# Where the first head's query weights wait, and how closely two blocks' units are set among the expert rows

## The reference, cut to what matters

```python
xn   = rmsnorm(x)                                    # x: 1024 tokens x 1024
proj = xn @ w_in                                     # columns of both branches and their gates
mix  = (sigmoid(g_sb) * y_sb @ W_sb + sigmoid(g_ml) * y_ml @ W_ml) @ w_out
h    = x + mix                                       # y_sb: stick-breaking attention, y_ml: mLSTM
# PEER: experts by product keys
q        = (rmsnorm(h) @ w_query).reshape(T, 8, 2, 128)
v1, i1   = top_k(q[:, :, 0] @ keys1[h].T, 16)        # 8 heads, 128 keys per half
v2, i2   = top_k(q[:, :, 1] @ keys2[h].T, 16)
top_s, c = top_k(v1[..., :, None] + v2[..., None, :], 16)
e        = i1[c // 16] * 128 + i2[c % 16]            # 8 heads x 16 = 128 experts per token
out      = h + sum_k softmax(top_s)_k * gelu(expert_u[e_k] . hn) * expert_v[e_k]
```

## Time and profile before

| | us |
|---|---|
| median of 3 executions | 3257.53 (3256.76 to 3258.34) |
| the profiled execution's own time | 3256.99 |
| its span, first to last instruction | 3254.8 |
| TensorE busy | 2583.9 (79%) |
| VectorE busy | 2067.9 (64%) |
| ScalarE, GpSimd busy | 1132.3, 1208.8 |
| moved by DMA | 1258.39 MB, 387 GB/s over the span |

### The profile page before, as it was taken

How to read it: one execution, slowest core, us unless ns; L and a number is a source line. 1 busy time by engine, 2 the same in 40 slices (tenths; PEclk the granted TensorE clock), 3 DMA queues, 4 the chain that set the end, 5 groups by cost and what they waited for, 6 DMA issues and landing times.

```text
span 3254.8 us, 40512 instructions
## 1 busy us (share of the span) xinstructions
PE 2583.9 (79%) x14592; PEld 1309.4 (40%) x14592; DVE 2067.9 (64%) x4792; ACT 1132.3 (35%) x3556; POOL 1208.8 (37%) x1048
## 2 busy tenths in 40 slices
PE   8997988998898788997787887899787555555555
PEld 6775544555364243553353333455353111111111
DVE  1324659777458788764448798775447857765544
ACT  3211435442323553332323474334132232233222
POOL 0002334333334453333334365333333444444443
PEclk9998999999999999999899999999998777777777
DMA  4455999999999999999999999999999999999998
GB/s 137 138 180 195 411 415 388 416 416 417 389 411 418 412 419 417 415 419 417 416 412 403 413 401 420 416 418 414 417 415 413 402 421 421 421 419 418 421 420 333
DMA packets 219287, 1258.39 MB, mean 387 GB/s; under 512 B 24272, under 2 KB 27344, under 8 KB 88016
## 3 DMA queue, kind: packets, MB, share of 16 engines
q0 software_dynamic: 147456, 1073.81, 80.1%
q1 hardware_dynamic: 64128, 161.56, 13.5%
q10 hardware_dynamic: 7504, 20.45, 1.6%
HBM read 1249.96 MB, written 5.77 MB: 386 GB/s over the span
## 4 chain that ended last, share of the span: by engine, by line
DMA 41%; PE 34%; DVE 9%; issue 6%; ACT 6%; POOL 3%; DVEq 0%; POOLq 0%; ACTq 0%; SPq 0%
DMA rowsb<-uv,e_idx 38%; PE yacc L975 13%; PE mixp L622 7%; DVE rowsb L1820 4%; PE mixp L647 4%; POOL rowsb L1046 3%; DMA wt<-w_query_ 3%; PE mixp L720 2%; ACT diag L1365 2%; ACT wg L1360 2%; PE mixp L634 1%; PE yacc L622 1%; DVE area L1464 1%; PE mixp L659 1%; ACT gmt L1346 1%
## 5 line engine op out<-in xcount | busy, mean ns | idle before, releaser
L1046 POOL DMA_INDIRECT rowsb<-uv,e_idx x1024 | 1204.6, 1176 | 2019.0 <-PE yacc L975 1583.3
L1820 DVE CUSTOM_DVE_ANT_0 rowsb<-rowsb,hnrow 128x1024 f32<-128x1024 f32 x1024 | 1242.1, 1222 | 843.7 <-DMA rowsb<-uv,e_idx 838.7
L975 PE MATMUL yacc<-rowsb,diag 64*64 64x512 f32 x8192 | 1196.0, 707 | 606.8 <-ACT diag L1365 587.7
L975 PEld LDWEIGHTS yacc<-rowsb,diag 64*64 64x64 f32 x8192 | 295.0, 148 | 1337.1 <-ACT diag L1365 908.7
L1346 ACT ACTIVATE gmt<-dots 128x2 f32<-128x2 f32 x512 | 104.1, 203 | 1585.5 <-DVE dots L1820 1571.5
L622 PE MATMUL mixp<-area,wt 128*128 128x256 f32 x2112 | 488.6, 385 | 1.3 <-ACT area L1101 1.2
L622 PEld LDWEIGHTS mixp<-area,wt 128*128 128x128 f32 x2112 | 392.6, 190 | 131.7 <-issue 82.8
L1365 ACT ACTIVATE diag<-ident,wg 128x64 f32<-128x64 f32 x1024 | 300.3, 340 | 16.7
L1360 ACT ACTIVATE wg<-gmt,gate 128x1 f32<-128x1 f32 x1024 | 245.5, 286 | 17.7
L647 PE MATMUL mixp<-area,wt 128*128 128x256 f32 x960 | 225.5, 388 | 6.4 <-DMA wt<-w_query_ 6.3
L1064 ACT ACTIVATE area<-mixp 128x512 f32<-128x512 f32 (+3 forms) x314 | 136.9, 482 | 268.2 <-PE mixp L622 136.8
(11 more groups left out here) (257 smaller groups left out, 1823.7 us busy)
## 6 DMA issues: line engine op xcount, KB each, us to landing
wt<-w_merge SPq DMA_DIRECT2D x96, 512.0 KB
wt<-w_feat SPq DMA_DIRECT2D x80, 512.0 KB
wt<-w_query_ SPq DMA_DIRECT2D x64, 512.0 KB
wt<-w_tok SPq DMA_DIRECT2D x32, 512.0 KB
rowsb<-uv,e_idx POOLq DMA_INDIRECT x1024
wt<-w_out_ SPq DMA_DIRECT2D x24, 512.0 KB
rowsb<-w_out_ SPq DMA_DIRECT2D x8, 512.0 KB, 4.7
area<-keysT ACTq DMA_DIRECT2D x16, 256.0 KB, 8.2
```

The source lines that it names most:

```text
L975: last = pe.matmul(yacc[at:at + HP, k % 2, c * NCH:(c + 1) * NCH], diag[r * HP:(r + 1) * HP, s, :], rowsb[r * HP:(r + 1) * HP, s, D + c * ...
L1046: pool.indirect_dma_start(rowsb[:, n % RS, :], None, uv, bass.IndirectOffsetOnAxis(ap=e_idx[:, i % 2, k:k + 1], axis=0)).then_inc(row_load ...
L1820: dve.tensor_tensor_reduce(rowsb[:, s, 0:D], rowsb[:, s, 0:D], hnrow[:, i % HR, :], 1.0, 0.0, ALU.mult, ALU.add, dots[:, s:s + 1]).then_in ...
```

## The change

It has three parts. First, `QRY[0]` and `QRY[1]` leave the ring of weights: SP loads them into place 7 of `rowsb`, right behind the `w_out` units, which move from places 4 to 7 down to places 3 to 6. Gather 3 now waits for the last use of `w_out`, and gather 7 for the last use of `QRY[1]`. The ring so holds `QRY[2]`, `QRY[3]` and `QRY[4]` where it held `QRY[0]` to `QRY[2]`. Second, block 0's remaining 14 query steps stand in slots 0, 1, 2, 3, 5, 6, 8, 9, 11, 12, 14, 15, 17 and 18. Third, the planner knows of these steps' load and sets only one step of block 1 before slot 19; block 1 now takes slots 16 to 101, where it took slots 11 to 107. Blocks 2 and 3 stand in the slots that they had. The parts of the third group of heads' search move one slot back (slots 12 to 20), those of the fourth start at slot 23, and a gate step moves from slot 20 to 22.

```diff
-RING = [(b, u) for b in range(NB) for u in UNITS if (b, u[0]) != (0, "out")]
+RING = [(b, u) for b in range(NB) for u in UNITS if b > 0 or (u[0] != "out" and u not in QRY[0:2])]
...
         def early_out(n):
-            return rowsb[:, RS // 2 + n // 2, n % 2 * D:(n % 2 + 1) * D]
+            return rowsb[:, 3 + n // 2, n % 2 * D:(n % 2 + 1) * D]
+
+        def early_query(n):
+            return rowsb[:, RS - 1, n * D:(n + 1) * D]
...
-            return [2.6, dve_, 5.1]
+            return [2.6 + 3.6 * steps[s][0], dve_, 5.1 + 1.3 * steps[s][0]]
...
                 while k < len(cost[b]) and (s % PP > 1 or s < PP):
+                    if k >= 1 and s <= REST_AT[-1]:
+                        break
...
-        N_REST = N_QRY - 5
-        for s in range(N_REST):
+        REST_AT = (0, 1, 2, 3, 5, 6, 8, 9, 11, 12, 14, 15, 17, 18)
+        assert len(REST_AT) == N_QRY - 5
+        for s in REST_AT:
             steps[s][0] = 1
         for b in range(1, NB):
-            lo = N_REST - 3 if b == 1 else NT * (b - 1) * PP - PP + BLOCK_END
+            lo = REST_AT[-1] - 2 if b == 1 else NT * (b - 1) * PP - PP + BLOCK_END
...
+                        if b == 0 and 4 + KD <= k < 6 + KD:
+                            n = k - 4 - KD
+                            sp.dma_start(early_query(n).rearrange("p (n c) -> p n c", n=4), head_query(n)).then_inc(firstq_loaded, 16)
                         yield
                     if b == 0:
                         yield
-                        for n in range(2):
-                            refill(b, QRY[n])
                         yield
...
+                    pe.wait_ge(firstq_loaded, 32)
                     for m in range(2):
-                        w = weights(0, QRY[m])
+                        w = early_query(m)
...
-                        if n == RS // 2:
+                        if n == 3:
                             ready(pool, ("o", 0, 3))
+                        if n == RS - 1:
+                            ready(pool, ("q0", 1))
```

More of the change, by code:

```diff
@@ L233, in build @@
         x_taken = [sem(f"x_taken{b}") for b in range(8)]
-        outw_loaded = sem("outw_loaded")
+        outw_loaded, firstq_loaded = sem("outw_loaded"), sem("firstq_loaded")
         w_loaded = [sem(f"w_loaded{u}") for u in range(WR)]
@@ L370, in unit_key @@
                 return ("o", b, 3), n + 1
-            if name == "qry" and b == 0 and n < 2:
-                return ("q0", 1), n + 1
             if name == "qry" and b == 0 and n < 4:
@@ L425, in build @@
         TOP_EACH, BLOCK_END = 9, 44
-        GATES = ((3, 0, 1, 1), (11, 0, 2, 2), (20, 0, 4, 2), (40, 0, 6, 2),
+        GATES = ((3, 0, 1, 1), (11, 0, 2, 2), (22, 0, 4, 2), (40, 0, 6, 2),
                  (62, 1, 0, 2), (65, 1, 2, 2), (74, 1, 4, 2), (84, 1, 6, 2))
@@ L442, in build @@
             i, p = divmod(n, PP)
-            if n < 20:
-                parts_at[i][p] = {0: 0, 1: 4, 2: 2, 3: 2, 4: 0, 5: 2, 6: 2, 7: 2}.get(n, 1)
+            if n < 21:
+                parts_at[i][p] = {0: 0, 1: 4, 2: 2, 3: 2, 4: 0, 5: 2, 6: 2, 7: 2, 11: 0}.get(n, 1)
             elif n < 40:
-                parts_at[i][p] = (n - 19) * TOP_EACH // 20 - (n - 20) * TOP_EACH // 20
+                parts_at[i][p] = max(0, n - 21) * TOP_EACH // 18 - max(0, n - 22) * TOP_EACH // 18
             else:
                 parts_at[i][p] = (n - 39) * N_PARTS // 43 - (n - 40) * N_PARTS // 43
+        steps = [[0] * NB for s in range(N_SLOT)]
         def slot_load(s):
@@ L476, in spread_ticks @@
             return placed, k
-        steps = [[0] * NB for s in range(N_SLOT)]
         N_HEAD = N_FIRST + 4
-        N_REST = N_QRY - 5
-        for s in range(N_REST):
+        REST_AT = (0, 1, 2, 3, 5, 6, 8, 9, 11, 12, 14, 15, 17, 18)
+        assert len(REST_AT) == N_QRY - 5
+        for s in REST_AT:
             steps[s][0] = 1
         for b in range(1, NB):
-            lo = N_REST - 3 if b == 1 else NT * (b - 1) * PP - PP + BLOCK_END
+            lo = REST_AT[-1] - 2 if b == 1 else NT * (b - 1) * PP - PP + BLOCK_END
             hi = NT * b * PP - PP + BLOCK_END
@@ L502, in _, with head_query @@
             def _(sp):
+                def head_query(k):
+                    k0, h0 = 4 * (k % 2), k // 2
+                    return w_query[:, k0:k0 + 4, 2 * h0 * P:2 * (h0 + 1) * P]
                 def load_unit(g):
@@ L530, in load_unit @@
                     elif b == 0 and k < 4:
-                        four = to.rearrange("p (n c) -> p n c", n=4)
-                        k0, h0 = 4 * (k % 2), k // 2
-                        ins = sp.dma_start(four, w_query[:, k0:k0 + 4, 2 * h0 * P:2 * (h0 + 1) * P])
+                        ins = sp.dma_start(to.rearrange("p (n c) -> p n c", n=4), head_query(k))
                     else:
```

## The result

The changed kernel takes 3291.9 us (median of 4 runs, 3286.4 to 3293.6) against 3257.2 for the kernel before (4 runs): the ratio is 1.0101, 95% interval 1.0089 to 1.0113, so it is 1.0% slower. The forecast had 3271.6.

What follows compares the result with a forecast made beforehand. DMA was taken as the bound: from about 325 us, time is bytes divided by rate. Terms -5.3 - 2.5 + 8.2 + 1 + 12.7 = +14.1 us on 3257.0 gave 3271.1, as a median 3271.6; range 3256 to 3283.

Steps and rivals of the forecast that it cites:

- What bounds the kernel: Whole kernel: from about 325 us on the time is bytes divided by rate, DMA at some 415 GB/s.
- (a): Head's end: the 10.44 us wait for `QRY[3]` goes, `add_rows` starts near 296.5; 5.3 us won, bounds 2.4 and 8.2.
- (b): Full stretch: two units of query weights are no longer moved there; 2.5 us won.
- The second part: Block 0's query steps spread out: changes nothing by itself with DMA saturated, counted as nothing; pushes block 1 to slot 16.
- (c): Attention, slots 29 to 37: 66.0 us long, 13.6 lost, 8.2 more than before, bounds 3 and 14.
- (d): Slots 38 to 47: TensorE 66.3 us against 65.5 of DMA, even; 1 us lost, bounds 0 and 4.
- (e): mLSTM, slots 48 to 63: 113.5 us against 100.8 of DMA; 12.7 us lost, bounds 7 and 16.
- the rival's paragraph: Rival on the mLSTM stage: run-ahead covers TensorE's excess, 3259; weighed against the skill's weight-load rule; chance 0.13.
- The block's end: Slots 83 to 85 instead of 89 to 91: the shortfall stands there with the same waits, as before.
- (1) to (3): Rivals: run-ahead covers TensorE's excess, 3259, chance 0.13; attention's excess absorbed too, 3250, 0.15; new stall in first slots, 3277, 0.10.

Runs made afterwards that it cites:

- experiment 1: The early query units alone, with the schedule's numbers put back to those of the kernel before: 3251.4 us, ratio 0.9977 to the kernel before.
- experiment 3: Changed kernel with block 0's last fourteen query units one per slot in slots 0 to 13, block 1 unmoved: 3285.6 us, 1.0089 to the kernel before.
- experiment 8: Changed kernel with nine search parts moved out of the attention steps, to slots 21 to 28 and 38: 3286.4 us, 1.0085 to the kernel before.
- experiment 6: Changed kernel with the gate projection's fourteen steps over slots 38 to 50, block 1 ending at slot 104: 3277.5 us, 1.0052 to the kernel before.
- experiment 4: Changed kernel with the steps of slots 38 to 47 dealt 1,1,1,1,1,1,2,1,2,3: 3287.3 us, 1.0093 to the kernel before.
- experiment 7: Changed kernel with slots 52, 57 and 62 left without a step, block 1 ending at slot 104: 3278.3 us, 1.0063 to the kernel before.
- experiment 9: Changed kernel with one output step in each of slots 78 to 84, block 1 ending at slot 103: 3284.1 us, 1.0083 to the kernel before.

## Why the prediction was wrong, point by point

- **What bounds the kernel**, and the measure of loss as rate short of 416 GB/s: right. Away from the stages named here both pages stand at 410 to 421 GB/s in most slices. That the measured terms add up to the difference of the spans is no proof of it, since both kernels move the same bytes (1258.39 and 1258.41 MB) and the sum must then come out; it shows that no stage was left out.
- **(a) and (b)**, right in mechanism, and alone in their sum: 7.8 forecast, 7.5 measured (experiment 1), though this is partly luck: there the head gave most of it, and the units next to nothing. In the changed kernel the head won 8.3 instead of 5.3, the upper bound: the term had left 2.9 us behind 310 us as belonging to the start of the loop, but with the query weights there and the first `add_rows` at 295.4 that shortfall went too (slots 0 to 3 lost 3.4 us before and 0.7 after). `add_rows` came 1.1 us earlier than the 296.5 of the forecast. In the ten other traces with the early units the head and slots 0 to 3 lose 3.1 to 6.2 us, so 5.3 lies just below what they win (6.2 to 9.3 against 12.4). The landing of `QRY[5]` was put too early: it took 11.0 us instead of 6 to 8, and the units behind it up to 19.2. TensorE waited 5.3 us for them in slots 0 to 3, 0.97 of it for `QRY[5]`, with little effect on the transfers: 0.7 us lost in these slots.
- **The second part** costs nothing by itself: shown by the rates up to slot 29 (experiment 3).
- **(c)** right: 68.0 us for 66.0, and 14.2 us lost for 13.6; +8.3 for +8.2 by the forecast's own count, +10.4 by the attention's slots alone. That VectorE's work sets this stage's length is shown by experiment 8.
- **(d)** is the step that failed: "10 x 5.53 + 3 x 3.65 = 66.3 us against 50.4 + 15.1 = 65.5 us of DMA. Even". The sum of TensorE's work was nearly right. It was taken as the stage's length, for ten slots in which TensorE would have had to be busy without a break. The ten slots took 77.6 us: 70.06 of work, 3 to 4 of them the price of `add_rows` at the lower clock (22.2 us for the stretch's 160 matmuls, where ten times 1.88 are 18.8), and 7.5 idle, all of it in four waits for `diag`, for which the term had nothing. Only 61.0 of the 65.5 us of transfers that the forecast counted fell into these 77.6 us, so 16.6 were lost, for the forecast's 1 with an upper bound of 4. Experiment 6 shows that 10 of them go once the steps have thirteen slots, with TensorE's waits still there: the step that failed is the balance of TensorE's time against the transfers in ten slots, and the waits and the clock were missing on TensorE's side. How much of the 10 belongs to the shared slots and how much to the room is open: experiment 4 only moved the shared slots, and experiment 6 changes both. In the five other traces with the same steps in these ten slots the loss is 14.0 to 17.0 us, so it is no chance of one trace. What the clock alone cost in the timed runs stays open.
- **(e)** right in mechanism: 115.5 us for 113.5, 369 GB/s for "near 370", and without three of the steps in these slots a little under half of the loss goes in the stage itself (experiment 7). That it came out at +12.7 exactly is luck: 3.3 us of the stage's length are slot 48's lower clock in this trace, and in four other traces with the same steps in slots 38 to 63 the stage lost 8.8, 10.8, 12.8 and 14.4 us. By the Trainium skill, "Perfetto Trace Analysis", section "Identifying the Most-Contended Engine", which judges TensorE's headroom by its share of the peak rate and by weight-load busy time, the latter would have shown room: it is 71.31 of 115.5 us here. TensorE had none, 115.47 of 115.5 busy and the transfers short, so the weighing against this rule in the rival's paragraph held.
- **The block's end**, "as before", was wrong by 4.7 us. The stretch lasts as long as before (45.9 and 45.8 us) with the same 35 us of TensorE's work, but the transfers lose more of it. With the output steps one per slot they lose 3.5 us (experiment 9), which fits a backlog that the closer steps had used up.
- **The rivals.** (1) to (3) did not come about. There is no new stall in slots 5 and 6.
- The 3.7 us behind slot 108 can't be put down to the change: the same stretch took between 2257.5 and 2262.3 us in the traces of the other kernels, and lost 9.3 to 13.7 of transfers in them (9.2 before, 12.9 in the changed kernel).
- The range ended at 3283, and even with every term at its own upper bound (-2.4 - 2.5 + 14 + 4 + 16) the forecast would have reached 3286.6. The bound of 4 us on (d) and the nothing for the block's end left no place for what happened. The losses are not independent either: a stage that ends with the queue empty leaves little to cover the waits of the next. The first three steps of the gate projection, one per slot, lost 2.1 us before and 6.6 behind the closer attention (experiment 6).

## What to carry to other kernels

When steps are pushed closer on an engine that feeds a saturated DMA queue, don't price a stage by that engine's busy time: add what it waits for inside each slot and the lower clock that can follow a wait, and compare the sum with the time of the transfers. Here 66.3 us of work against 65.5 of transfers looked even, and took 77.6. Ask of every known wait what hid it: a wait "as before" can cost more once the backlog ahead of it is gone. And try the parts of a change apart, since here a head worth 7.5 us came together with a schedule that cost 43.

## What the runs showed of the hardware

A short wait can cost TensorE more than its length, and not the same each time. The same instructions begin slot 48 behind the same wait of 2.46 us in the changed kernel and in that of experiment 3. TensorE's timeline in the changed kernel:

```profile
618.53 2.68 PE L984 MATMUL yacc<-rowsb,diag 64*64 64x512 f32 x16 [2.46 <-ACT diag L1376]
...
624.59 4.54 PE L729 MATMUL mixp<-area,wt 128*128 128x256 f32 x16
```

and in that of experiment 3:

```profile
615.28 1.95 PE L987 MATMUL yacc<-rowsb,diag 64*64 64x512 f32 x16 [2.46 <-ACT diag L1379]
...
618.97 3.62 PE L732 MATMUL mixp<-area,wt 128*128 128x256 f32 x16
```

The slot took 10.52 us in the one and 7.24 in the other. The sums by stretch give the granted clock. It was 0.60 from 618.5 to 624 us in the changed kernel, so mostly the lower level (1.2 GHz):

```profile
618.50:624.00 5.50, 5.46 (x22) 2.44 (x23) 0.64 (x2) 2.43 (x6) 1.87 (x2) 0.60 1.03 425
```

and 1.00 (2.4 GHz) in the other:

```profile
615.30:619.00 3.70, 3.70 (x25) 1.89 (x26) 0.57 (x2) 2.37 (x6) 1.17 (x2) 1.00 1.01 422
```

Eight kernels have these instructions in slot 48 behind the same wait of 2.46 us. In their traces, one of each, the slot took 7.24 us three times, 8.89 once, 10.52 twice and 12.21 twice. Slot 38 shows the same: `add_rows` took 3.69 us behind a wait of 1.59 in the changed kernel and 1.95 behind the same wait in experiment 3. The Trainium skill, "TensorE: Matmul & The Clock Gate", section "HAM oscillation — how this bites in real kernels", tells of a matmul kernel that falls back to the lower clock at every wait for data. The traces here agree in that a fall comes right behind a wait, in this case one for another engine, with the difference that the same wait brings it in some traces and not in others. In the changed kernel and that of experiment 3 this made 5 us between stages with the same instructions (3.3 in slot 48 and 1.7 in slot 38), more than some of the repairs above were worth.
